# A product-key expert layer: one gather for both expert tables, and its work handled choice by choice

## The chip, the cores and the metric

The kernel runs on one core of one Trainium2 chip. The metric is the device time of one execution in microseconds, taken as a median over executions. A core has TensorE (PE: matrix multiplies, with the weight load shown apart as PEld), VectorE (DVE), ScalarE (ACT), GpSimd (POOL), SyncE (SP, which here only issues transfers), and 16 DMA engines that move data between device memory and the on-chip buffers.

## The reference, cut to what matters

Two layers of a backbone run on 128 prompt tokens and 512 latent tokens, together five blocks of 128 tokens. Each layer has a token mixer and then PEER, an expert layer with 128 x 128 = 16384 tiny experts. For every token and every one of 8 heads, two lists of 128 scores are cut to their best 16, the 256 sums of pairs are cut to the best 16, and the 16 experts so chosen give one row of `u_tab` and one of `v_tab` each:

```python
def one(xb):                                  # a block of 128 tokens
    q = (xb @ wq).reshape(PEER_BLOCK, PEER_HEADS, 2, PEER_HALF)
    s = jnp.einsum('thpd,hpnd->thpn', q, keys).astype(jnp.float32)
    s_top, i_top = lax.top_k(s, PEER_TOPK)    # PEER_TOPK = 16
    cand = s_top[:, :, 0, :, None] + s_top[:, :, 1, None, :]
    cand_idx = i_top[:, :, 0, :, None] * PEER_N_KEYS + i_top[:, :, 1, None, :]
    best, pos = lax.top_k(cand.reshape(...), PEER_TOPK)
    idx = jnp.take_along_axis(cand_idx.reshape(...), pos, axis=-1)
    g = jax.nn.softmax(best, axis=-1)
    ue = jnp.take(u_tab, idx, axis=0)         # rows of 1024 float32 = 4 KB
    ve = jnp.take(v_tab, idx, axis=0)
    act = jax.nn.gelu(jnp.einsum('td,thkd->thk', xb, ue), approximate=False)
    return jnp.einsum('thk,thkd->td', (g * act), ve)
```

Five blocks, 8 heads, 16 choices and 2 layers make 1280 choices of 128 rows each in either table.

## The kernel before, in words

The function `experts` is one stage, run once a layer. Its work is cut into 40 units, unit n being one head and one block of tokens (`where(n)`: n // 5 and n % 5). Tokens lie across the 128 partitions. A unit has 16 choices s. There are five roles, one an engine:

- PE computes queries (`ask`, one job for two blocks), scores of the two lists (`score`, three units ahead, `LEAD = 3`) and the weighted sums. `sums(n, s)` multiplies a 128 x 128 diagonal matrix, whose diagonal holds the weight of choice s for each token, with the 128 gathered v rows, and accumulates in one of two PSUM tiles `ps_y`.
- DVE picks the 16 experts of a unit in `choose(n)` (some 22 instructions, many of which wait for the one before through the semaphore `dve_steps`), takes the dot product of the gathered u row with the token's own row (line 1834), forms the weights (lines 1838, 1840) and adds the finished `ps_y` to `y_tok` (`gather_sum`, line 1742).
- ACT takes the softmax exponentials (line 1924), the gelu of a unit's 16 dot products in one instruction (line 1928), copies the next unit's token rows to PSUM (line 1899), and builds the diagonals, one a choice (line 1935).
- POOL issues the gathers, one indirect DMA of 128 rows of 4 KB at a time (line 1637). It does nothing else until the tail of the stage.
- SP issues the plain transfers: the query weights of the next head, and at the end of the stage the loads that the next stage starts with.

The order within a unit is written out by hand. DVE does the 16 dot products of unit n, waits for gelu, forms the 16 weights, runs the whole of `choose(n + 2)`, and then `gather_sum(n - 1)`; then come the dot products of unit n + 1. Only when the weights of the unit are there does ACT start on its diagonals, and PE on its sums. So the v rows of a unit are wanted one unit later than its u rows, and POOL issues them so: two gathers of u rows of unit n, two of v rows of unit n - 1, in turn. The u rows have eight slots of 4 KB a partition in two buffers named `ring`, the v rows eight in two buffers named `early`. POOL waits for `u_used` (a dot product is done) before it issues into a u slot, and for `v_used` (a sum is done) before a v slot. POOL handles its instructions strictly in order, so a wait for a slot of one kind also holds back the gathers of the other.

In the last two units DVE also works on the end of the layer between dot products (`behind_dot`: residual, layer norm). After the last unit follow the rest of that, and in the first layer the modulation of the new rows and their transposes on PE (`new_turn`) for the next stage.

## Time and profile before

| what | value |
|---|---|
| median of 3 executions | 6708.51 us (6702.12 to 6709.55) |
| span of the profiled execution | 7135.4 us |
| instructions in it | 94928 |
| mean granted clock of TensorE in it, as a share of full speed | 0.931 |
| gathered by POOL's queue | 1342.34 MB in the two expert stages |

The page gives no other time for the profiled execution than its span, so everything outside the first and last instruction is not seen. The profiled execution is 427 us longer than the median of the unprofiled ones. In the forty slices of the page (178 us each) the two expert stages are the slices 10 to 20 and 29 to 40, where GB/s is near 355; the token mixers lie before each. A line number such as L1637 is a line of the kernel. "Idle before" in brackets names what ended the wait by the semaphore events.

### The profile page before, as it was taken

Reading aid. Unit: us, or ns where it says so; the run is one execution under the profiler, and the core shown is the slowest. Engines: PE = TensorE matmul, PEld = TensorE weight load, DVE = VectorE, ACT = ScalarE, POOL = GpSimd, SP = SyncE. Lnnn points to the kernel's source line nnn. Section 1 sums busy time; section 2 is a strip of 40 time slices with the busy share of each in tenths; the row PEclk is TensorE's granted clock in tenths of the full one; section 3 lists DMA queues with packets and bytes.
Section 4 is the critical chain, followed back from the end, with each engine's and each line's share of the span. In section 5 each row is a group of like instructions: output and inputs, shape, how many; then the busy total and the mean of one; then the engine's idle time right before and its main releaser. Section 6 shows DMA issues by size and latency. Waiting matters only on the chain. (4 is left out here: it accounts for less than half of the span.)

```text
span 7135.4 us, 94928 instructions
## 1 busy us (share of the span) xinstructions
PE 5756.5 (81%) x36912; PEld 4065.6 (57%) x36912; DVE 4044.6 (57%) x8218; ACT 1880.9 (26%) x3574; POOL 2797.2 (39%) x2909
## 2 busy tenths in 40 slices
PE   7889999795777777777788899997867777777776
PEld 7779999593333333333387799986833333333332
DVE  3654334557665666566636634346576566656666
ACT  1662112412222122212226621124121222122211
POOL 0330000014666666666613300000166666666665
PEclk8999999997998999999999999999988999999999
DMA  4002121327999999999921012222389999999998
GB/s 173 17 33 84 72 75 69 144 99 287 355 354 352 361 351 358 357 357 364 387 85 39 23 72 83 75 81 90 107 329 351 357 357 357 347 355 355 353 372 318
DMA packets 425299, 1632.88 MB, mean 229 GB/s; under 512 B 47648, under 2 KB 69600, under 8 KB 412260
## 3 DMA queue, kind: packets, MB, share of 16 engines
q0 software_dynamic: 368640, 1342.34, 49.4%
q1 hardware_dynamic: 56214, 284.46, 10.9%
q8 instruction: 297, 4.87, 0.3%
q14 instruction: 148, 1.21, 0.1%
HBM read 1611.68 MB, written 17.56 MB: 228 GB/s over the span
## 5 line engine op out<-in xcount | busy, mean ns | idle before, releaser
L1984 PE MATMUL ex_ps_y<-early,peer_small 128*128 128x512 f32 x5120 | 2534.4, 643 | 887.5 <-DMA early<-in_peer_v,ex_index 626.0
L1984 PEld LDWEIGHTS ex_ps_y<-early,peer_small 128*128 128x128 f32 x5120 | 993.4, 204 | 2348.5 <-issue 1416.5
L1834 DVE CUSTOM_DVE_ANT_0 ring<-ring,ex_ps_h 128x1024 f32<-128x1024 f32 x1280 | 1510.6, 1219 | 696.3 <-DMA ring<-in_peer_u,ex_index 545.1
L1637 POOL DMA_INDIRECT early<-in_peer_v,ex_index x1280 | 1234.7, 965 | 792.8 <-issue 355.8
L1637 POOL DMA_INDIRECT ring<-in_peer_u,ex_index x1280 | 1219.8, 953 | 706.5 <-issue 369.8
L1935 ACT ACTIVATE peer_small<-ident,ex_w 128x128 f32<-128x128 f32 x1280 | 441.2, 392 | 1477.2 <-PE ex_ps_y L1984 707.7
L1117 POOL TENSOR_SCALAR ring<-ring 128x2048 f32<-128x2048 f32 x2 | 10.8, 5387 | 1623.7 <-DMA ring<-mod_rows 1623.7
L258 PE MATMUL conv_ps<-h_high,conv_wh 128*128 128x320 f32 x1024 | 317.1, 310 | 9.3 <-DVE conv_wl L156 9.3
L258 PE MATMUL conv_ps<-h_low,conv_wh 128*128 128x320 f32 x1024 | 316.6, 309 | 0.0
L258 PE MATMUL conv_ps<-h_high,conv_wl 128*128 128x320 f32 x1024 | 316.5, 309 | 0.0
L1928 ACT ACTIVATE ex_act<-ex_dot 128x16 f32<-128x16 f32 x80 | 17.2, 216 | 1116.0 <-issue 944.7
L1965 PE MATMUL ex_ps_q<-h_high,ex_wh 128*128 128x256 f32 (+1 forms) x768 | 255.4, 333 | 57.7 <-DVE h_low L156 29.4
L258 PE MATMUL rf_ps<-rf_wh,h_high 128*128 128x256 f32 x960 | 268.2, 279 | 14.0 <-DVE rf_wl L156 14.0
L258 PE MATMUL rf_ps<-rf_wl,h_high 128*128 128x256 f32 x960 | 267.7, 279 | 0.0
L258 PE MATMUL rf_ps<-rf_wh,h_low 128*128 128x256 f32 x960 | 267.6, 279 | 0.0
L1965 PE MATMUL ex_ps_q<-h_low,ex_wh 128*128 128x256 f32 (+1 forms) x768 | 238.5, 311 | 26.5 <-issue 26.2
L1965 PE MATMUL ex_ps_q<-h_high,ex_wl 128*128 128x256 f32 (+1 forms) x768 | 239.7, 312 | 24.4 <-issue 24.1
L1038 POOL TENSOR_TENSOR room<-room,rec_bounds 128x256 f32<-128x256 f32 x80 | 64.7, 809 | 437.6 <-ACT room L1032 437.3
L1965 PEld LDWEIGHTS ex_ps_q<-h_high,ex_wh 128*128 128x128 f32 x768 | 171.0, 223 | 68.5 <-issue 37.9
L156 DVE TENSOR_TENSOR rf_wl<-ring,rf_wh 128x2048 fp32r<-128x2048 f32 (+1 forms) x36 | 74.7, 2085 | 238.5 <-ACT rf_wh L285 238.5
L156 DVE TENSOR_TENSOR conv_wl<-ring,conv_wh 128x2048 fp32r<-128x2048 f32 (+1 forms) x42 | 91.7, 2188 | 203.1 <-ACT conv_wh L285 203.1
L258 PEld LDWEIGHTS conv_ps<-h_high,conv_wh 128*128 128x128 f32 x1024 | 193.5, 189 | 9.8 <-DVE conv_wl L156 9.8
(335 smaller groups left out, 12091.3 us busy)
## 6 DMA issues: line engine op xcount, KB each, us to landing
ring<-in_w_in SPq DMA_DIRECT2D x54, 2048.0 KB, 7.8
ring<-in_mod_w SPq DMA_DIRECT2D x22, 2048.0 KB, 7.6
ring<-in_w_branch SPq DMA_DIRECT2D x12, 2048.0 KB, 7.8
ring<-in_peer_u,ex_index POOLq DMA_INDIRECT x1280
early<-in_peer_v,ex_index POOLq DMA_INDIRECT x1280
room<-in_peer_wq SPq DMA_DIRECT2D x14, 1024.0 KB
ring<-in_w_out SPq DMA_DIRECT2D x4, 2048.0 KB, 8.3
room<-mod_rows SPq DMA_DIRECT2D x12, 512.0 KB, 7.9
```

The source lines that it names most:

```text
L156: return nc.vector.tensor_tensor(low, full, high.bitcast(F32), ALU.subtract)
L258: last = nc.tensor.matmul(ps[:, at:at + cols], lhs, rhs, start=k == 0 and n == 0, stop=k == KT - 1 and n == 2)
L1038: step(nc.gpsimd.tensor_tensor(kk[:, m, at], kk[:, m, at], lb[:, 1, at], ALU.mult))
L1117: step(P_.tensor_scalar(vec[:, :, 1, :], vec[:, :, 1, :], 1.0, None, ALU.add))
L1637: nc.gpsimd.indirect_dma_start(rows[slot], None, table, bass.IndirectOffsetOnAxis(ap=index[n % 4][:, s:s + 1], axis=0)).then_inc(arrived[s ...
L1834: V.tensor_tensor_reduce(out=row, in0=row, in1=ps_h[:], scale=1.0, scalar=0.0, op0=ALU.mult, op1=ALU.add, accum_out=dot[n % 2][:, s:s + 1] ...
L1928: act.activation(act_v[n % 2][:], dot[n % 2][:], ACT.Gelu).then_inc(gelu_done, 1)
L1935: act.activation(diag[s % DIAGS], ident[:], ACT.Copy, scale=wgt[n % 2][:, s:s + 1]).then_inc(diag_ready, 1)
L1965: last = nc.tensor.matmul(ps_q[:, a, 0:width], w[h % 2][:, k, w_cols], h_split[x][:, k, toks], start=k == 0 and m == 0, stop=k == KT - 1 a ...
L1984: last = nc.tensor.matmul(ps_y[n % 2][:, c:c + 512], diag[s % DIAGS], v_row[s % V_SLOTS][:, c:c + 512], start=s == 0, stop=s == TOPK - 1)
```

## The change

The two tables are joined on the host into one, `peer_uv`, whose row holds the u row and then the v row of an expert: 8 KB. A choice takes one gather instead of two. The sixteen slots of 4 KB become eight of 8 KB in the same four half buffers; a slot is taken from the issue of its gather until its sum is done on PE, so POOL waits for `v_used` alone. `choose` is cut into 16 parts, and part s of `choose(n + 2)` stands behind the dot product s of unit n (parts 0 and 1 both behind the second). The softmax is divided by its sum ahead of time (`soften` on ACT, `shares` on DVE). Gelu, weight and diagonal are made choice by choice on ACT: three instructions for each dot product, each waiting for the one before. PE's query job is cut in two, its scores come one choice later, and the v sums of a unit run right behind the dot products of the same unit rather than one unit later. At the end of the stage the loads for the next one and the transposes move behind the last sums.

```diff
-        U_SLOTS = V_SLOTS = DIAGS = 8
-        u_row, v_row = ([room[:].rearrange("p k n -> p (k n)")[:, s * D:(s + 1) * D] for room in rooms for s in range(4)] for rooms in (ring, early))
+        SLOTS = DIAGS = 8
+        pair_row = [room[:].rearrange("p k n -> p (k n)")[:, s * 2 * D:(s + 1) * 2 * D] for room in (*ring, *early) for s in range(2)]
+        u_row, v_row = ([row[:, side * D:(side + 1) * D] for row in pair_row] for side in range(2))
...
-                def gather(rows, arrived, table, n, s):
-                    slot = s % len(rows)
-                    nc.gpsimd.indirect_dma_start(rows[slot], None, table, bass.IndirectOffsetOnAxis(
-                        ap=index[n % 4][:, s:s + 1], axis=0)).then_inc(arrived[slot], 16)
-
-                for n in range(units + 1):
-                    if n < units:
-                        pool.wait_ge(routed, n + 1)
-                    for s in range(0, TOPK, 2):
-                        if n < units:
-                            if TOPK * n + s >= U_SLOTS:
-                                pool.wait_ge(u_used, TOPK * n + s + 2 - U_SLOTS)
-                            pool.sem_inc(going, 1)
-                            for j in (s, s + 1):
-                                gather(u_row, u_in, T["peer_u"], n, j)
-                        if n:
-                            if TOPK * (n - 1) + s >= V_SLOTS:
-                                pool.wait_ge(v_used, TOPK * (n - 1) + s + 2 - V_SLOTS)
-                            pool.sem_inc(going, 1)
-                            for j in (s, s + 1):
-                                gather(v_row, v_in, T["peer_v"], n - 1, j)
+                for n in range(units):
+                    pool.wait_ge(routed, n + 1)
+                    for s in range(TOPK):
+                        if TOPK * n + s >= SLOTS:
+                            pool.wait_ge(v_used, TOPK * n + s + 1 - SLOTS)
+                        pool.sem_inc(going, 1)
+                        nc.gpsimd.indirect_dma_start(pair_row[s % SLOTS], None, T["peer_uv"], bass.IndirectOffsetOnAxis(
+                            ap=index[n % 4][:, s:s + 1], axis=0)).then_inc(uv_in[s % SLOTS], 16)
...
+                def choose(n, part):
+
+                    def chosen(step, ins):
+                        ins.then_inc(dve_steps, 1)
+                        assert step <= CHOICE_STEPS
+
+                    def behind(step):
+                        dve.wait_ge(dve_steps, n * CHOICE_STEPS + step)
+
+                    full = [P, 2, TOPK, TOPK]
+                    lo = 0 if part < 4 else 8
+                    if part == 0:
+                        dve.wait_ge(scored, n + 1)
+                        V.tensor_copy(lists[:], ps_s[:, 0:2 * P].rearrange("p (a n) -> p a n", a=2)).then_inc(listed, 1)
+                    if part == 1:
+                        dve.wait_ge(listed, n + 1)
+                    if part == 3:
+                        behind(2)
+                    if part in (1, 3):
+                        dve.sem_inc(picking, 1)
+                        lo = 0 if part == 1 else 8
...
+                    if part == 15:
+                        behind(14)
+                        chosen(15, V.scalar_tensor_tensor(num[:, 0], num[:, 0], float(P), num[:, 1], ALU.mult, ALU.add))
+                        behind(15)
+                        V.tensor_scalar(index[n % 4][:], num[:, 0], base[:, bass.ds(l, 1)], None, ALU.add).then_inc(routed, 1)
+
+                def shares(n):
+                    dve.wait_ge(soft_done, n + 1)
+                    if n >= 2:
+                        dve.wait_ge(weighed, TOPK * (n - 1))
+                    V.reciprocal(total[n % 2][:], total[n % 2][:]).then_inc(recip_done, 1)
+                    dve.wait_ge(recip_done, n + 1)
+                    V.tensor_scalar(share[n % 2][:], soft[n % 2][:], total[n % 2][:], None, ALU.mult).then_inc(share_ready, 1)
...
-                        row = u_row[s % U_SLOTS]
-                        dve.wait_ge(u_in[s % U_SLOTS], (l * units + n) * 32 + 16 * (s // U_SLOTS + 1))
+                        row = u_row[s % SLOTS]
+                        dve.wait_ge(uv_in[s % SLOTS], (l * units + n) * 32 + 16 * (s // SLOTS + 1))
                         V.tensor_tensor_reduce(out=row, in0=row, in1=ps_h[:], scale=1.0, scalar=0.0, op0=ALU.mult,
-                                               op1=ALU.add, accum_out=dot[n % 2][:, s:s + 1]).then_inc(u_used, 1)
+                                               op1=ALU.add, accum_out=dot[n % 2][:, s:s + 1]).then_inc(dotted, 1)
+                        if n == 0 and s == 1:
+                            head_low_of(4)
+                            shares(0)
+                        if n + 2 < units:
+                            if s == 1:
+                                choose(n + 2, 0)
+                            if s:
+                                choose(n + 2, s)
+                        if s == 7 and n + 1 < units:
+                            shares(n + 1)
+                        if n == 0 and s == 9:
+                            low(1)
+                        if s == 11 and b == NB - 1 and h + 2 < PH:
+                            low(h + 2)
                         behind_dot(n, s)
...
-                    dve.wait_ge(gelu_done, n + 1)
-                    V.reciprocal(total[n % 2][:], total[n % 2][:]).then_inc(recip_done, 1)
-                    dve.wait_ge(recip_done, n + 1)
-                    V.scalar_tensor_tensor(wgt[n % 2][:], act_v[n % 2][:], total[n % 2][:], soft[n % 2][:], ALU.mult, ALU.mult).then_inc(w_ready, 1)
-                    if n == 0:
-                        head_low_of(4)
-                        low(1)
-                    if n + 2 < units:
-                        choose(n + 2)
                     if n and n < units - 1:
                         gather_sum(n - 1)
...
+                def soften(n):
+                    act.wait_ge(centred_done, n + 1)
+                    if n >= 2:
+                        act.wait_ge(share_ready, n - 1)
+                    act.activation(soft[n % 2][:], centred[n % 4][:], ACT.Exp, accum_out=total[n % 2][:]).then_inc(soft_done, 1)
...
+                soften(0)
                 for n in range(units):
                     h, b = where(n)
-                    act.wait_ge(routed, n + 1)
-                    act.activation(soft[n % 2][:], centred[n % 4][:], ACT.Exp, accum_out=total[n % 2][:])
-                    if n == units - 1:
-                        roots(3, 0, 3)
-                    act.wait_ge(u_used, TOPK * (n + 1))
-                    act.activation(act_v[n % 2][:], dot[n % 2][:], ACT.Gelu).then_inc(gelu_done, 1)
                     if n + 1 < units:
-                        rows_of(n + 1)
-                    act.wait_ge(w_ready, n + 1)
+                        soften(n + 1)
                     for s in range(TOPK):
-                        if TOPK * n + s >= DIAGS:
-                            act.wait_ge(v_used, TOPK * n + s + 1 - DIAGS)
-                        act.activation(diag[s % DIAGS], ident[:], ACT.Copy, scale=wgt[n % 2][:, s:s + 1]).then_inc(diag_ready, 1)
-                        if s == TOPK // 2 - 2:
-                            if n and n + LEAD < units and where(n + LEAD)[1] % 2 == 0:
-                                turn(n + LEAD)
-                        if s == TOPK // 2:
-                            if b == 2 and h + 2 < PH:
-                                high(h + 2)
+                        r, at = TOPK * n + s, slice(s, s + 1)
+                        act.wait_ge(dotted, r + 1)
+                        if s == TOPK - 1 and n + 1 < units:
+                            rows_of(n + 1)
+                        act.activation(act_v[n % 2][:, at], dot[n % 2][:, at], ACT.Gelu).then_inc(gelu_done, 1)
+                        if s == 0:
+                            act.wait_ge(share_ready, n + 1)
+                        act.wait_ge(gelu_done, r + 1)
+                        act.activation(wgt[n % 2][:, at], act_v[n % 2][:, at], ACT.Copy, scale=share[n % 2][:, at]).then_inc(weighed, 1)
+                        act.wait_ge(weighed, r + 1)
+                        if r >= DIAGS:
+                            act.wait_ge(v_used, r + 1 - DIAGS)
+                        act.activation(diag[s % DIAGS], ident[:], ACT.Copy, scale=wgt[n % 2][:, at]).then_inc(diag_ready, 1)
+                        if s == 9 and n and n + LEAD < units and where(n + LEAD)[1] % 2 == 0:
+                            turn(n + LEAD)
+                        if s == 10 and b == 2 and h + 2 < PH:
+                            high(h + 2)
+                        if s == 12 and n == units - 1:
+                            roots(4, 0, 4)
...
-                    pe.wait_ge(v_in[s % V_SLOTS], (l * units + n) * 32 + 16 * (s // V_SLOTS + 1))
+                    pe.wait_ge(uv_in[s % SLOTS], (l * units + n) * 32 + 16 * (s // SLOTS + 1))
                     pe.wait_ge(diag_ready, TOPK * n + s + 1)
                     for c in (0, 512):
-                        last = nc.tensor.matmul(ps_y[n % 2][:, c:c + 512], diag[s % DIAGS], v_row[s % V_SLOTS][:, c:c + 512], start=s == 0, stop=s == TOPK - 1)
+                        last = nc.tensor.matmul(ps_y[n % 2][:, c:c + 512], diag[s % DIAGS], v_row[s % SLOTS][:, c:c + 512], start=s == 0, stop=s == TOPK - 1)
...
-                        if s == 2 and n and n + LEAD < units and where(n + LEAD)[1] % 2 == 0:
-                            ask(n + LEAD)
-                        if s == TOPK - 4 and n + LEAD < units:
+                        if s in (2, 5) and n and n + LEAD < units and where(n + LEAD)[1] % 2 == 0:
+                            ask(n + LEAD, (0,) if s == 2 else (1,))
+                        if s == TOPK - 3 and n + LEAD < units:
                             score(n + LEAD)
                         sums(n, s)
-                        if goes_on and n == units - 1 and s in (8, 11):
-                            new_turn((s - 8) // 3)
-                for b in range(2, NB) if goes_on else ():
+                for b in range(NB) if goes_on else ():
...
-        "peer_u": a["peer_u"].reshape(DEPTH * EXPERTS, D), "peer_v": a["peer_v"].reshape(DEPTH * EXPERTS, D),
+        "peer_uv": np.concatenate([a["peer_u"], a["peer_v"]], axis=-1).reshape(DEPTH * EXPERTS, 2 * D),```

The order of the instructions on POOL, in the middle of the first expert stage. Before (`ring` holds u rows, `early` v rows, `ex_index` the row numbers of a unit):

```order
L1637 DMA ring_6<-in_peer_u,ex_index_396 128x1024 x2
L1637 DMA early_387<-in_peer_v,ex_index_395 128x1024 x2
L1637 DMA ring_6<-in_peer_u,ex_index_396 128x1024 x2
L1637 DMA early_387<-in_peer_v,ex_index_395 128x1024 x2
L1637 DMA ring_7<-in_peer_u,ex_index_396 128x1024 x2
```

And in the changed kernel:

```order
L1643 DMA ring_6<-in_peer_uv,ex_index_388 128x2048 x2
L1643 DMA ring_7<-in_peer_uv,ex_index_388 128x2048 x2
L1643 DMA early_379<-in_peer_uv,ex_index_388 128x2048 x2
L1643 DMA early_380<-in_peer_uv,ex_index_388 128x2048 x2
L1643 DMA ring_6<-in_peer_uv,ex_index_388 128x2048 x2
```

Two kinds of gathers of two neighbouring units became one kind of one unit, half as many and twice as wide.

On DVE, at the end of a unit before: the last dot products (L1834, two rows each), the weights, and the start of the whole choice:

```order
L1834 ISA ring_7,ex_dot_403<-ring_7,ex_ps_h 128x1024
L1834 ISA ex_dot_403 128x1
L1838 RECIPROCAL ex_total_409<-ex_total_409 128x1
L1840 SCALAR_TENSOR_TENSOR ex_w_411<-ex_act_405,ex_total_409,ex_soft_407 128x16
L1674 COPY peer_small<-ex_ps_s 128x256
L1679 MAX ex_top<-peer_small 128x8 x2
L1683 MAX_INDEX ex_topi<-ex_top,peer_small 128x8
L1685 MATCH_REPLACE peer_small<-ex_top,peer_small 128x128
L1683 MAX_INDEX ex_topi<-ex_top,peer_small 128x8
L1685 MATCH_REPLACE peer_small<-ex_top,peer_small 128x128
```

And in the changed kernel around the seam of two units, where L1876 is the dot product and L1776 the finished sum of a unit:

```order
L1735 TENSOR_REDUCE ex_num<-peer_small 128x32
L1876 ISA early_380,ex_dot_395<-early_380,ex_ps_h 128x1024
L1876 ISA ex_dot_395 128x1
L1738 SCALAR_TENSOR_TENSOR ex_num<-ex_num 128x16
L1740 TENSOR_SCALAR ex_index_389<-ex_num,ex_base 128x16
L1776 COPY main<-ex_ps_y_417 128x1024
L1876 ISA ring_6,ex_dot_394<-ring_6,ex_ps_h 128x1024
L1876 ISA ex_dot_394 128x1
L1876 ISA ring_6,ex_dot_394<-ring_6,ex_ps_h 128x1024
L1876 ISA ex_dot_394 128x1
L1672 COPY peer_small<-ex_ps_s 128x256
```

The block of the choice between two units is gone; between two dot products stand at most four instructions of it.

On ACT, across a unit's end before (L1928 gelu, L1899 the token rows, L1935 the diagonals):

```order
L1935 ACTIVATE peer_small<-ident,ex_w_410 128x128 x7
L1924 ACT_TABLE_LOAD
L1924 ACTIVATE ex_soft_407,ex_total_409<-ex_centred_401 128x16
L1928 ACT_TABLE_LOAD
L1928 ACTIVATE ex_act_405<-ex_dot_403 128x16
L1899 ACTIVATE ex_ps_h<-room_2 128x1024
```

And in the changed kernel (L1979 gelu, L1983 weight, L1987 diagonal of one choice, L1947 the exponentials):

```order
L1941 ACTIVATE ex_ps_h<-room_2 128x1024
L1979 ACTIVATE ex_act_397<-ex_dot_395 128x1
L1983 ACTIVATE ex_w_405<-ex_act_397,ex_share_403 128x1
L1987 ACTIVATE peer_small<-ident,ex_w_405 128x128
L1947 ACT_TABLE_LOAD
L1947 ACTIVATE ex_soft_399,ex_total_401<-ex_centred_393 128x16
L1979 ACT_TABLE_LOAD
```

One gelu of 16 values became 16 of one value, with a weight instruction behind each; the two table loads of a unit are still two.

## Rows read from the trace of the kernel before

**Rows 1.** The page: busy time by engine.

```profile
PE 5756.5 (81%) x36912; PEld 4065.6 (57%) x36912; DVE 4044.6 (57%) x8218; ACT 1880.9 (26%) x3574; POOL 2797.2 (39%) x2909
```

**Rows 2.** Windows (start:end, length, busy by engine, clock, DMA share, GB/s): both gather stretches.

```profile
1648.00:3572.00 1924.00, 1439.30 (x3820) 676.79 (x3821) 1226.69 (x2855) 403.25 (x913) 1235.16 (x1282) 0.92 0.95 359
5188.00:7106.00 1918.00, 1428.47 (x3793) 670.22 (x3793) 1217.27 (x2837) 402.75 (x914) 1220.60 (x1276) 0.92 0.94 357
```

**Rows 3.** DMA queues in 1648:3572: packets, MB, share.

```profile
q0 software_dynamic: 184293, 671.09, 91.8%
q1 hardware_dynamic: 8976, 17.83, 2.6%
```

**Rows 4.** Windows inside one unit, 2309 to 2353.

```profile
2309.00:2315.00 6.00, 4.60 (x11) 1.82 (x10) 1.82 (x7) 0.62 (x2) 1.88 (x2) 1.00 1.02 408
2315.00:2318.00 3.00, 2.01 (x5) 0.57 (x3) 2.58 (x9) 2.04 (x7) 1.88 (x2) 1.00 0.58 176
2318.00:2324.00 6.00, 3.97 (x8) 1.35 (x8) 5.90 (x12) 0.49 (x2) 4.18 (x5) 1.00 0.87 308
2331.00:2353.00 22.00, 16.81 (x40) 6.90 (x40) 9.00 (x16) 5.31 (x10) 15.06 (x16) 0.99 1.02 408
```

**Rows 5.** Timeline of POOL: start, length, line, [idle before <-releaser].

```profile
2310.31 0.94 POOL L1637 DMA_INDIRECT ring<-in_peer_u,ex_index  x1 [0.30 <-issue]
2315.55 0.94 POOL L1637 DMA_INDIRECT early<-in_peer_v,ex_index  x1 [4.31 <-PE ex_ps_y L1984]
```

**Rows 6.** Timeline of DVE in the same unit: last dot, weights, choice, sum, first dot.

```profile
2301.78 1.22 DVE L1834 CUSTOM_DVE_ANT_0 ring<-ring,ex_ps_h 128x1024 f32<-128x1024 f32 x1
...
2303.64 0.42 DVE L1674 COPY peer_small<-ex_ps_s 128x256 f32<-128x256 f32 x1
...
2311.90 0.18 DVE L1687 CAST ex_topf<-ex_topi 128x32 f32<-128x32 uint32 x1 [4.52 <-remote]
...
2319.41 1.21 DVE L1742 TENSOR_TENSOR main<-main,ex_ps_y 128x1024 f32<-128x1024 f32 x1
2320.54 1.22 DVE L1834 CUSTOM_DVE_ANT_0 ring<-ring,ex_ps_h 128x1024 f32<-128x1024 f32 x1
```

**Rows 7.** Timeline of ACT in the next unit.

```profile
2334.70 1.28 ACT L1928 ACT_TABLE_LOAD   x1
2347.59 0.21 ACT L1928 ACTIVATE ex_act<-ex_dot 128x16 f32<-128x16 f32 x1 [11.61 <-issue]
2347.72 1.01 ACT L1899 ACTIVATE ex_ps_h<-room 128x1024 f32<-128x1024 f32 x1
```

**Rows 8.** Timelines: DVE, one hop from ACT; ACT, a diagonal.

```profile
7082.28 0.16 DVE L1838 RECIPROCAL ex_total<-ex_total 128x1 f32<-128x1 f32 x1 [0.28 <-ACT ex_act L1928]
...
2330.10 0.40 ACT L1935 ACTIVATE peer_small<-ident,ex_w 128x128 f32<-128x128 f32 x1 [5.79 <-issue]
```

**Rows 9.** Timeline of PE: the last sums of the program, back to back.

```profile
7089.64 22.91 PE L1984 MATMUL ex_ps_y<-early,peer_small 128*128 128x512 f32 x53
```

**Rows 10.** Windows: plain loads of 16 KB a partition, at the program's start.

```profile
5.00:20.00 15.00, 7.55 (x140) 6.45 (x144) 8.95 (x4) 2.12 (x2) 0.00 (x0) 1.00 1.01 429
```

**Rows 11.** Windows where TensorE had idled.

```profile
2375.00:2378.00 3.00, 0.00 (x0) 0.00 (x0) 3.00 (x6) 0.00 (x0) 2.31 (x3) 1.00 1.06 410
2378.00:2381.00 3.00, 2.67 (x4) 0.68 (x4) 1.09 (x3) 0.00 (x0) 2.17 (x3) 0.74 1.04 422
2381.00:2384.00 3.00, 1.21 (x3) 0.66 (x3) 1.42 (x4) 2.89 (x5) 2.39 (x3) 0.50 1.03 420
```

**Rows 12.** DVE and POOL at the ends of the stages.

```profile
3594.99 1.22 DVE L1781 TENSOR_TENSOR main<-main,ring 128x1024 f32<-128x1024 f32 x1
3599.34 1.22 DVE L156 TENSOR_TENSOR h_low<-ex_ps_h,h_high 128x1024 fp32r<-128x1024 f32 x1 [3.12 <-ACT h_high L1947]
...
7120.01 1.28 DVE L1775 SCALAR_TENSOR_TENSOR room<-room,ex_root,room 128x1024 f32<-128x1024 f32 x1
...
L1664 POOL TENSOR_TENSOR main<-main,ring x2: 3200/3212/3224, 3568.7 to 3582.4; 128x1024 f32<-128x1024 f32 x2
```

154 lines of the change are left out of this document (85 added, 69 removed).

## The prediction

> **What bounds the kernel now.** I read the page's busy shares first: PE 81%, DVE 57%, POOL 39% [rows 1]. No engine is full over the span, so the answer must come from a stage. The stages that the change touches are the two gather stretches. In windows over them, the DMA engines are busy 95% and 94% of 1924 and 1918 us, at 359 and 357 GB/s, while PE has 1439 us of work (36.0 us for each of 40 units), DVE 1227 (30.7) and ACT 403 (10.1) [rows 2]. 671.09 MB of the 688.9 MB moved there are gathered rows [rows 3]. That looks like a transfer limit, but the average hides two levels. Inside one unit the engines hold 408 GB/s for 22 us at a stretch, and then comes a hole: 176 GB/s for 3 us, 308 for the next 6 [rows 4]. So the transfers are the bound only in the good part of a unit, and something makes the holes.
>
> The hole has a cause in the order. POOL waited 4.31 us for a sum on PE before it could issue into a v slot, and every u gather behind it stood too [rows 5]. PE had no diagonals, since ACT's gelu waits for all 16 dot products of the unit. And DVE, after its last dot product at 2301.78, is away with weights, choice and sum until 2320.54, of which 4.52 us are a wait in the middle of the choice [rows 6]: 17.6 us without a dot product, in which eight u slots of 0.52 MB fill in 10 us and then stand full. The bound is a transfer rate of 408 GB/s with a hole of each unit in it: 16.78 MB at 408 take 41.1 us, and a stretch of 1924 us for 40 units is 48.1.
>
> **The change part by part.**
>
> Bytes stay the same: 1280 gathers of 1 MB for 2560 of half that. At the rate of the good part, 688.9 MB / 408 GB/s = 1688 us a stage. Nothing in the trace shows a gather of 8 KB rows. Plain loads of 16 KB a partition ran at 429 GB/s over 15 us [rows 10]. At that rate the stage would take 1606 us. I take 408, the row for the same queue and kind, and keep 429 as the far end; on the bad side a gather of 8 KB rows could be no faster per instruction than two of 4 KB, which is 408 again.
>
> POOL: 0.94 us a gather and 0.30 between two [rows 5], so 32 x 1.24 = 39.7 us a unit before and 19.8 now. If a row of 8 KB counts as two rows, the instruction is 1.88 us and the unit 34.9, still below 41. This is a gain in room, not in time.
>
> Dot products and choice: the instructions are the same, 30.7 us of DVE a unit. A part of the choice is at most four short instructions; the biggest pieces are some 1.3 us, and with a dot product of 1.22 [rows 6] that is 2.5 us, against 1688 / 640 = 2.64 us a choice. Waits of a part for the part before it fall behind a dot product, and so cost nothing. What is queued behind a waiting part is the next dot product, and behind that ACT, PE and the slot. I price that by the 8 slots below.
>
> ACT: 16 gelu instructions instead of one and 16 weight instructions are new. From 0.21 us for a gelu, the same for a weight, 0.40 for a diagonal and 0.28 for a hop of a semaphore [rows 7, 8], a choice takes 0.21 + 0.28 + 0.21 + 0.28 + 0.40 + 0.28 = 1.7 us, below 2.64. A copy begins right behind a gelu with no table load between [rows 7], so alternating gelu and copy brings none. Two table loads of 1.28 us a unit stay, and now stand in front of the first choice of a unit: some 3 us, once a unit.
>
> PE: a sum is four passes, 22.91 / 53 = 0.43 us each, 1.73 us [rows 9]. All its work is 36.0 us a unit, below 42, and its half jobs of queries now delay one sum by 3 us rather than by 6.
>
> Slots: a row of 8 KB is held after landing for dot product 1.22, hop 0.28, ACT 1.7 and sum 1.73, about 5 us. Eight slots go round in 8 x 2.64 = 21 us, which leaves 16 us for the transfer, so six gathers stay in flight. A stall of DVE, ACT or PE of 5 to 8 us is covered; one of 11 us would leave a hole, and a few may. That replaces what went: I see nothing late next but the transfer itself.
>
> Start of a stage: DVE does head work and all of `choose(1)` before its first dot product, while the eight slots take 20 us to fill. I add 7 us. So 1695 us a stage against 1924, a gain of 229, or 458 for both.
>
> End of a stage: before, DVE and POOL did most of the tail beside v gathers and sums of the last unit. Now the last dot product follows the last landing, and then come two normal rows, two modulations, the sum, residual 4 and the low parts, some 34 us of DVE, where it was 28 after 3572 (to 3599.34) [rows 12]; POOL's four operations of 3.2 us each and the two transposes that wait for them follow the modulations. I add 12 us in the first layer. The second layer had a drain of PE alone (22.91 us [rows 9]) and its end hangs on the same seven operations of DVE up to 7120.01 [rows 12]: plus 4. The loads for the next stage are issued some 15 us before the last sum instead of some 45, and need 10, so they are covered; if not, they cost 5.
>
> Sum: 7135.4 - 458 + 16 = about 6693 us for a profiled execution, 442 less. The median of the runs shown is 427 us less than that span, and the trace doesn't say where. If the whole execution shrinks alike, the gain is 442 x 0.94 = 415 and the time 6293. If the waits shrink and the byte-bound time can't, a stretch of before is 1924 x 0.94 = 1809, the new one 1695, and the gain 2 x 114 - 16 = 212: 6497. I take the middle, 6400.
>
> The Trainium skill speaks against all this. Its page "DMA: Bandwidth & Descriptors", section "Bandwidth", puts the limit for transfers from device memory at about 358 GB/s a core, and says that for these "the HBM side (~358) binds". The averages of 359 and 357 GB/s would be just that limit, and the change would gain nothing. But 408 GB/s over 22 us and 429 over 15 us stand in this trace [rows 4, 10], so by the rows the limit is higher for this core alone.
>
> **The rivals.**
>
> No change. The average rate is a ceiling over long stretches, and the 408 GB/s are bursts that the holes pay for. For it: both stretches agree within 0.6% [rows 2]. Against: each hole has an engine in it that waits for a slot [rows 5], which a ceiling wouldn't need. By the rule of the page this is what would come. The time would be 6708.5 + 16, or, with ends hidden, 6700.
>
> Half the gain. Some holes come back. The 4.52 us wait in the choice has no cause in the order [rows 6]; if such a stall strikes DVE, ACT and PE in turn, each a few times in two units, the eight slots run empty now and then, since every choice now goes through all three in series. The gain halves: 106 to 208, 6500 to 6600.
>
> More than forecast. Wider rows run at 429 GB/s: 82 us a stage more, 164 both, so 6240 from the middle.
>
> Slower: TensorE's clock. Where PE had idled, the granted clock fell from 1.00 to 0.50 [rows 11], the level of 1.2 GHz. Now sums come singly, 1.73 us of work and 0.9 us of pause, for 40 units. At 1.2 GHz all the time PE would need 72 us a unit against 48.1 now: 80 x 24 = 1900 us more. It decides from about a third of the time at the low level: 36 + 12 = 48. Against it: in the 22 us of 408 GB/s PE also works in pieces (16.81 of 22 us) and the clock is 0.99 [rows 4]; and a late PE has more work waiting, which fills its pauses. A small share of it would give 6750 to 6900.
>
> That the change doesn't do what it says is excluded by the order of instructions, which shows the halved gathers and the parts between dot products.
>
> **How the numbers follow.** Forecast (the holes close, rate near 408) 0.72, with its own range 6290 to 6500. More than forecast 0.10. Half the gain 0.10. No change 0.03. Slower 0.05. A difference under 0.2% (13 us) can't be told from none. Faster is 0.72 + 0.10 + 0.10 and a little of the rest, 0.92; same 0.02; slower 0.06. The range goes down half way to 6115, which is the fully scaled gain together with 429 GB/s, and up to the edge of the half gain: 6200 to 6600.
>
> **What would show it.** Right: in the gather stretches DMA share 1.0 and 400 GB/s or more in nearly every slice; stretches near 1700 us; DVE's main wait is for the landing of a row, at each choice; POOL waits mostly for sums on PE, with 640 gathers a stage of about 0.94 us. Wrong: slices near 358 GB/s with POOL never waiting would mean the ceiling; a mean clock well under 0.9 in the stretch with PE full would mean the slow rival; POOL waiting for PE while DMA share is below 0.95 would mean that eight slots are too few.

## The result

The changed kernel takes 6634.47 us (6628.62 to 6640.34, median of 4 runs), the kernel before beside it 6705.32 (6697.67 to 6709.55): ratio 0.9894, 95% interval 0.988 to 0.9908. It is faster by 71 us, 1.1%, where about 308 were forecast, and the time lies outside the range given. The profiled execution of the changed kernel has a span of 6626.6 us and a time of 6628.62: here profile and timing agree, as they did not for the kernel before, whose profiled execution was 427 us longer than the median. That gap is what the study is about. **On some occasions every execution of the kernel before takes 7103 to 7175 us (medians 7122 to 7158), on others 6697 to 6714 (medians 6702 to 6705), and by its span of 7135.4 us the profile shown ahead of the prediction belongs to the first sort.** An occasion is a set of runs of several kernels made one after another on one chip; the two sorts are called the slow and the fast level below. No profile of the kernel before was kept from the other.

The page of the changed kernel, busy time by engine and then the gather queue of the whole program (packets, MB, share of 16 engines):

```profile
PE 5624.5 (85%) x36912; PEld 3969.9 (60%) x36912; DVE 3985.8 (60%) x8216; ACT 2568.0 (39%) x6050; POOL 1574.6 (24%) x1629
...
q0 software_dynamic: 184320, 1342.26, 49.1%
```

Against [rows 1] POOL has fallen from 2797 to 1575 us (1280 instructions fewer), ACT has gained 687 us for 2476 instructions more, PE and DVE are nearly as they were.

Windows of the changed kernel over the first gather stretch (columns as in [rows 2]):

```profile
1653.00:1700.00 47.00, 35.87 (x118) 20.58 (x119) 37.93 (x106) 18.86 (x51) 20.87 (x21) 0.86 0.89 355
1700.00:3320.00 1620.00, 1332.63 (x3706) 602.70 (x3705) 1150.90 (x2747) 726.56 (x2100) 591.90 (x620) 0.97 1.01 415
3320.00:3340.00 20.00, 5.10 (x19) 3.32 (x17) 19.76 (x13) 3.33 (x3) 10.48 (x4) 0.64 0.20 80
```

The stretch is 1667 us long, not 1924 [rows 2], and 1620 us of it run at 415 GB/s with the DMA engines full. The 408 GB/s of [rows 4] were no burst. The Trainium skill's page "DMA: Bandwidth & Descriptors", section "Bandwidth", has about 358 GB/s for each of two cores that stream from the same memory domain, and a measured 425 GB/s for a 16 MB transfer on one core with its neighbour idle. This kernel runs on one core, and its trace is near the second figure, with 415 GB/s over 1620 us. The prediction took the 358 without that condition.

What DVE and POOL waited for between 2000 and 3000 us (engine, tile and line, releaser: us in total, times, longest):

```profile
DVE early L1876 <- DMA early<-in_peer_uv,ex_index: 162.7, 187, 2.1
DVE ring L1876 <- DMA ring<-in_peer_uv,ex_index: 120.4, 152, 2.1
POOL early L1643 <- PE ex_ps_y L2035: 299.5, 183, 3.7
POOL ring L1643 <- PE ex_ps_y L2035: 281.4, 159, 4.7
```

DVE waits for landings, choice by choice and never over 2.1 us; the 17.5 us without a dot product [rows 6] are gone. The same view of the kernel before:

```profile
DVE ring L1834 <- DMA ring<-in_peer_u,ex_index: 150.7, 58, 10.2
DVE peer_small L1674 <- remote: 89.9, 16, 10.6
DVE ring L1834 <- issue: 43.6, 21, 4.1
DVE ex_topf L1687 <- remote: 24.4, 7, 4.9
```

Here is the sign that the prediction had in one row only, the 4.52 us at line 1687 [rows 6]: waits whose releaser is "remote" (a signal came, but no instruction ended just before it) or "issue" (nothing that the profile shows was waited for). DVE has 182 us of them in 1000, the longest of 10.6 us. In the changed kernel it has none. That they are not waits of the order can be read at the longest. The copy at line 1674 waits for PE's scores alone (the semaphore `scored`), and PE had ended them 17 us before (timelines, windows 2004 to 2006 and 2020 to 2024):

```profile
2004.95 0.61 PE L1977 MATMUL ex_ps_s<-room 128*128 128x128 f32 x4
2022.92 0.42 DVE L1674 COPY peer_small<-ex_ps_s 128x256 f32<-128x256 f32 x1 [10.61 <-remote]
```

At each of the 16 copies with such a wait the scores had been done for 7.8 us or more. These waits are called stalls below: an engine starts late although what it waits for is done.

A choice on ACT at the end of the stage (timeline: start, length, line, [idle before <-releaser]), and POOL at its start, with the hole that eight full slots make before the first sum:

```profile
3309.33 0.20 ACT L1979 ACTIVATE ex_act<-ex_dot 128x1 f32<-128x1 f32 x1 [1.20 <-DVE ex_dot L1876]
3309.56 0.29 ACT L1983 ACTIVATE ex_w<-ex_act,ex_share 128x1 f32<-128x1 f32 x1
3309.89 0.40 ACT L1987 ACTIVATE peer_small<-ident,ex_w 128x128 f32<-128x128 f32 x1
```

```profile
1662.74 0.94 POOL L1643 DMA_INDIRECT early<-in_peer_uv,ex_index  x1 [0.30 <-issue]
1676.94 0.94 POOL L1643 DMA_INDIRECT ring<-in_peer_uv,ex_index  x1 [13.26 <-PE ex_ps_y L2035]
```

A choice costs ACT 0.96 us from gelu to the end of the diagonal. The gather instruction takes 0.94 us as before [rows 5], for a row of 8 KB as for one of 4 KB.

### The profile page after: what moved, and what is told of

Its sections match the earlier page's. It is cut to its first block and busy times, and to the rows that moved or that the text cites. A ratio compares the mean times of both kernels' runs of the same rounds, so it can differ in the third digit from the quotient of the medians.

```text
span 6626.6 us, 97627 instructions
## 1 busy us (share of the span) xinstructions
PE 5624.5 (85%) x36912; PEld 3969.9 (60%) x36912; DVE 3985.8 (60%) x8216; ACT 2568.0 (39%) x6050; POOL 1574.6 (24%) x1629
## 3 DMA queue, kind: packets, MB, share of 16 engines
q0 software_dynamic: 184320, 1342.26, 49.1%
## 5 line engine op out<-in xcount | busy, mean ns | idle before, releaser
L2035 PE MATMUL ex_ps_y<-ring,peer_small 128*128 128x512 f32 x2560 | 1261.5, 636 | 290.9 <-ACT peer_small L1987 290.7
L2035 PE MATMUL ex_ps_y<-early,peer_small 128*128 128x512 f32 x2560 | 1222.7, 608 | 292.4 <-ACT peer_small L1987 287.6
L2035 PEld LDWEIGHTS ex_ps_y<-ring,peer_small 128*128 128x128 f32 x2560 | 488.6, 201 | 1021.7 <-issue 1020.3
L1876 DVE CUSTOM_DVE_ANT_0 early<-early,ex_ps_h 128x1024 f32<-128x1024 f32 x640 | 780.5, 1221 | 516.9 <-DMA early<-in_peer_uv,ex_index 516.5
L2035 PEld LDWEIGHTS ex_ps_y<-early,peer_small 128*128 128x128 f32 x2560 | 451.4, 190 | 972.7 <-issue 972.4
L1876 DVE CUSTOM_DVE_ANT_0 ring<-ring,ex_ps_h 128x1024 f32<-128x1024 f32 x640 | 780.5, 1220 | 407.5 <-DMA ring<-in_peer_uv,ex_index 400.2
L1643 POOL DMA_INDIRECT ring<-in_peer_uv,ex_index x640 | 623.8, 975 | 1151.0 <-PE ex_ps_y L2035 913.7
L1979 ACT ACTIVATE ex_act<-ex_dot 128x1 f32<-128x1 f32 x1280 | 256.9, 201 | 1595.8 <-DVE ex_dot L1876 1594.9
L1643 POOL DMA_INDIRECT early<-in_peer_uv,ex_index x640 | 606.7, 948 | 1021.5 <-PE ex_ps_y L2035 984.6
L1987 ACT ACTIVATE peer_small<-ident,ex_w 128x128 f32<-128x128 f32 x1280 | 514.0, 402 | 42.0
L1983 ACT ACTIVATE ex_w<-ex_act,ex_share 128x1 f32<-128x1 f32 x1280 | 376.8, 294 | 46.4
L156 DVE TENSOR_TENSOR rf_wl<-ring,rf_wh 128x2048 fp32r<-128x2048 f32 (+1 forms) x36 | 74.7, 2086 | 242.4 <-ACT rf_wh L285 242.4
```

What stands on the lines that cost most here:

```text
L156: return nc.vector.tensor_tensor(low, full, high.bitcast(F32), ALU.subtract)
L1643: nc.gpsimd.indirect_dma_start(pair_row[s % SLOTS], None, T["peer_uv"], bass.IndirectOffsetOnAxis(ap=index[n % 4][:, s:s + 1], axis=0)).th ...
L1876: V.tensor_tensor_reduce(out=row, in0=row, in1=ps_h[:], scale=1.0, scalar=0.0, op0=ALU.mult, op1=ALU.add, accum_out=dot[n % 2][:, s:s + 1] ...
L1979: act.activation(act_v[n % 2][:, at], dot[n % 2][:, at], ACT.Gelu).then_inc(gelu_done, 1)
L1983: act.activation(wgt[n % 2][:, at], act_v[n % 2][:, at], ACT.Copy, scale=share[n % 2][:, at]).then_inc(weighed, 1)
L1987: act.activation(diag[s % DIAGS], ident[:], ACT.Copy, scale=wgt[n % 2][:, at]).then_inc(diag_ready, 1)
```

## The experiments

Four questions, in the order in which they came up. Each kernel is compared with the kernel before on the same occasion. Edits are shortened to the lines that matter. Where dots and sums run on 64 of 1024 columns, or a choice is left out, the text of the expectation or of the edit says so.

**1. Which part of the change brings the gain?** All four on one occasion, on which the kernel before took 7157.78 us (7137.2 to 7175.48).

Two 4 KB gathers a choice, all of the new order kept:

```diff
-  indirect_dma_start(pair_row[s % SLOTS], None, T["peer_uv"], ...index[n % 4][:, s:s + 1]).then_inc(uv_in[s % SLOTS], 16)
+  for row, table in ((u_row, "peer_u"), (v_row, "peer_v")):
+      indirect_dma_start(row[s % SLOTS], None, T[table], ...index[n % 4][:, s:s + 1]).then_inc(uv_in[s % SLOTS], 16)
```

> The changed kernel with its gathers undone alone: each choice takes two gathers of 4 KB rows from the two tables into the halves of its slot; the order of all engines stays. Three theories of why 442 us were expected and 71 came. P: the profile itself slows a stream of 4 KB packets (it records each), the holes of the profiled execution of before are not there in timed runs, and the stage of before stood at a transfer limit already; then this kernel's profiled span is far above its timed runs (6850 or more against 6650 to 6700). O: the order made the difference in the profile, and a timed run of before has smaller holes for another reason; then the profiled span is within 30 us of the timed runs, and both are near 6640. R: the 71 us are the rate of 8 KB rows (415 against about 405 GB/s); then the timed runs are at 6690 to 6710, whatever the profile says.

Measured: 7116.54 us (7108.66 to 7124.15), ratio 0.9954 (0.9938 to 0.997). None of the three theories has that time. Theory P falls besides: the profiled execution took 7108.66 us, in the range of the others, and for every kernel run here it is within 21 us of the median. So profiling doesn't make the gap.

The changed kernel with dots and sums on 64 of 1024 columns (`row[:, 0:64]`, `v_row[..][:, 0:64]`), once with 8 KB gathers and once with 4 KB gathers as above:

> The changed kernel with dot products and sums over 64 of the 1024 columns only (it leaves out the rest of both), so that no engine but the DMA ones is near its limit in the stage. All theories: the transfer limit for 8 KB rows, 6570 to 6630 timed, if the changed kernel (6634) stands at it. If it is below 6500, the changed kernel is held by its engines and not by transfers.

> The same with two gathers of 4 KB rows a choice (the same columns left out). P and R: the limit for 4 KB rows is higher than for 8 KB rows, by 30 to 80 us of timed time, and before (6705) stands within 30 us above it. O: as floor8 within 10 us, so that before has 60 us and more of holes in timed runs. P besides: the profiled span is above the timed runs by 200 us or more, though nothing but transfers can bound it.

Measured: 6623.17 (6610.37 to 6632.86) with 8 KB, 7073.17 (7060.05 to 7085.98) with 4 KB; ratios 0.9259 (0.9238 to 0.9281) and 0.9893 (0.9869 to 0.9916). The first is as expected; the second is 370 us or more above what any theory had.

The kernel before with the choice left out from the third unit on, so that DVE is hardly away between two units:

```diff
+  if n >= 2:
+      V.tensor_scalar(centred[n % 4][:], best[:], best[:, 0:1], None, ALU.subtract)
+      for _ in range(CHOICE_STEPS):
+          dve.sem_inc(dve_steps, 1)
+      V.tensor_scalar(index[n % 4][:], num[:, 0], base[:, bass.ds(l, 1)], None, ALU.add).then_inc(routed, 1)
+      return
```

> The kernel before with the choice between two units left out from the third unit on (it takes the experts of unit 1 again, and computes none of the rest), so the block of 11 to 16 us on DVE between dot products shrinks to some 2 us. P: timed within 20 us of 6705, since the block is hidden there. O: 40 us or more below 6705. In the profile the holes shrink in both, or stay if they are the profile's own: below 6800 if the order makes them even there, above 7000 if it doesn't.

Measured: 7127.19 (7115.75 to 7137.79), ratio 0.996 (0.9942 to 0.9978). DVE's stalls are what they were, 182.3 us of 1000 against 182.0, and the profiled time stayed above 7000 us, which the expectation kept for holes that the order doesn't make.

Windows 2000 to 3000 us of the four: `a4k`, `floor4`, `floor8`, `b_nochoice`:

```profile
2000.00:3000.00 1000.00, 773.02 (x2070) 362.16 (x2071) 617.84 (x1517) 401.42 (x1149) 649.12 (x681) 0.92 0.96 361
```

```profile
2000.00:3000.00 1000.00, 345.76 (x1390) 299.96 (x1390) 281.37 (x1521) 391.31 (x1143) 653.38 (x688) 0.54 0.96 365
```

```profile
2000.00:3000.00 1000.00, 386.78 (x1598) 331.68 (x1598) 322.00 (x1745) 453.69 (x1314) 391.48 (x392) 0.54 1.01 418
```

```profile
2000.00:3000.00 1000.00, 756.34 (x2067) 358.74 (x2066) 463.32 (x804) 216.60 (x485) 636.01 (x674) 0.92 0.94 358
```

With less than half of the work on PE and DVE (346 and 281 us for 773 and 618) the transfer stays at 365 GB/s as long as there are two gathers a choice, and is at 418 with one, so the low average is no ceiling on the transfers either. The new order with the old gathers gains 0.5%, the old order without its block on DVE 0.4%. The changed kernel itself was not run beside these; on another slow occasion it takes 6633 (question 2). So on this level the single gather is nearly the whole gain, and the holes that the prediction laid to the order have another cause.

**2. Is it the width of the row, or the number of gathers?** One occasion, kernel before 7121.52 us (7108.74 to 7162.69). First the changed kernel itself:

> The changed kernel as it is, beside the kernel before on this chip. Theory W (the wide gather is worth some 480 us wherever gathers of 4 KB run at 360 GB/s): on a chip where the kernel before takes 7120 to 7180 us this takes 6620 to 6650, ratio 0.925 to 0.932; on a chip where the kernel before takes 6705 it takes 6634, ratio 0.989. Theory Z (the changed kernel has the same two levels as the kernel before): the ratio stays at 0.989 on every chip, so about 7080 where the kernel before takes 7158.

Measured: 6632.69 (6625.63 to 6638.29), ratio 0.931 (0.9272 to 0.9349). The changed kernel shows no second level: 6634 where the kernel before takes 6705, 6633 where that takes 7122. DVE's stalls in it on this slow occasion sum to 1.7 us of 1000.

Then, on 64 of 1024 columns, a second gather beside each 8 KB gather, of rows of 64 B from a small table, with the same indices:

```diff
   indirect_dma_start(pair_row[s % SLOTS], None, T["peer_uv"], ...)
+  indirect_dma_start(tiny[s % SLOTS][:], None, T["peer_tiny"], ...index[n % 4][:, s:s + 1]).then_inc(uv_in[s % SLOTS], 16)
```

> The kernel with dots and sums on 64 of 1024 columns and 8 KB gathers (6623 us), and beside each of its gathers a second one of rows of 64 B from a small table: as many gather instructions and descriptors as with 4 KB gathers, 0.8% more bytes. Theory I (twice the gather instructions on GpSimd leave no room to make up for a stall: 64 of 1.24 us in a unit of 41 us): 7030 to 7100 us, as with 4 KB gathers. Theory S (the size of the row decides, not the number of gathers): 6620 to 6690, the descriptors of 64 B adding at most 1% to the transfers.

(The 64 in it should read 32: a unit has 16 choices.) Measured: 7032.14 (7029.73 to 7045.14). All the bytes but 0.8% move in rows of 8 KB, and the time is near that of 4 KB gathers. The width of the row is refuted as the cause, the number of gathers stands.

Four slots in place of eight with the 4 KB gathers, so that half as many are in flight:

> The same kernel with two 4 KB gathers a choice (7073 us with eight slots, so sixteen gathers in flight) and four slots: eight gathers of 4 KB in flight, as many gathers as the changed kernel has, half its bytes. Theory C (sixteen gathers outstanding stall GpSimd's queue and with it the other engines): 6620 to 6700, the stalls gone. Theories S and I: 7060 to 7200, no better, perhaps worse because fewer bytes are in flight.

Measured: 7108.32 (7105.31 to 7126.36), against 7073 with eight slots on another occasion. Fewer in flight is no cure; theory C falls.

The changed kernel with half the bytes, one 4 KB gather a choice:

> The changed kernel with half the bytes: rows of 4 KB that hold the first 512 columns of both experts, one gather a choice; the dot and the two matmuls of a choice keep their sizes. With a transfer of 4 KB at 360 GB/s it takes 23 us of a unit, so the engines set the unit. Theory S (rows of 4 KB bring stalls of 2 to 8 us on all engines wherever they are): the stalls are seen here too, DMA below its rate in over 10% of the slices though asked for half, 5500 to 6000 us. Theory I: no such stalls, GpSimd with room, 5100 to 5500 us. Both: with the transfers out of the way the next bound of a unit is DVE, ScalarE and TensorE at some 29 to 33 us.

Measured: 5931.92 (5915.66 to 5935.37). No wait on "remote" appears on DVE or POOL between 2000 and 3000 us, so 1280 gathers of 4 KB are as quiet as 1280 of 8 KB. The time by itself lies in the range of theory S (5500 to 6000), and the 5500 us of theory I were too low by 430; it is the trace that speaks for I, without the stalls and with PE as the bound, at 946 of 1000 us busy.

```profile
2000.00:3000.00 1000.00, 946.38 (x2836) 472.76 (x2836) 883.25 (x2115) 555.08 (x1607) 469.95 (x476) 0.98 0.78 265
```

**3. The number of rows, or of instructions?** On a first occasion the kernel before took 6704.37 us, the other level, on which the question can't be put. All on 64 of 1024 columns: the second gather with 16 rows in place of 128, the second gather beside every other choice only (`if s % 2:`), and, with no second gather, two small multiplications on GpSimd behind each gather.

```diff
-  indirect_dma_start(tiny[s % SLOTS][:], None, T["peer_tiny"], ...index[n % 4][:, s:s + 1])
+  indirect_dma_start(tiny[s % SLOTS][0:16, :], None, T["peer_tiny"], ...index[n % 4][0:16, s:s + 1])
```

> As the kernel with a second gather of 64 B rows beside each 8 KB gather (7032 us; 6623 without it), but the second gather fetches 16 rows on 16 partitions instead of 128: as many gather instructions on GpSimd (32 a unit), but 9 descriptors for every 8 as without it, instead of 16. Theory I (what counts is that GpSimd issues without a pause, about 1.24 us each): about 7030, unless the smaller gather is issued much faster, then in proportion. Theory D (what counts is the number of rows, thus descriptors and packets): 6640 to 6690.

> The second gather of 128 rows of 64 B only beside every other choice: 24 gathers in a unit instead of 16 (6623 us) or 32 (7032). Theory D (each gather of 128 rows costs its descriptors, in proportion): half of the 409 us, 6810 to 6850. Theory I (GpSimd has to be without a pause; 24 x 1.24 = 29.8 us of a unit of 41): 6620 to 6680.

> No second gather; in its place two multiplications of a tile of 128 columns on GpSimd behind each gather, each waited for, by the row of 0.81 us for 256 columns some 0.4 us each with their waits 1.0 to 1.2 us: GpSimd as full as with 32 gathers a unit, with 16 gathers. Theory I (a full GpSimd, whatever it does): 6950 to 7100 us. Theory D or any theory of the gathers themselves: 6620 to 6660.

Measured: 6635.43 (6616.6 to 6644.28), 6644.24 (6632.91 to 6647.05) and 6908.75 (6907.8 to 6921.68). The last one, which neither theory has, tells nothing of the stalls: it has none on DVE, and it was not run on the slow level. It is slow for a reason of its own. Its gathers stand 2.72 us apart, 0.98 for the gather and the rest for the two multiplications and their waits, so GpSimd's own chain needs 43.5 us for the 16.78 MB of a unit, which is 386 GB/s; 383 were measured.

On a second occasion the kernel before took 7128.56 us (7103.09 to 7155.4):

> Again the second gather of 128 rows of 64 B beside each 8 KB gather (7032 us on chip 11). Where the kernel before takes 7120 to 7160: 7030 to 7050. Where it takes 6705: if the level belongs to the chip and not to the kernel, 6640 to 6700.

> Again the second gather with 16 rows (6635 us on chip 4). Where the kernel before takes 7120 to 7160: 7000 to 7050 if the number of gather instructions counts (theory I), 6640 to 6690 if the number of rows does (theory D). Where it takes 6705: 6635 again, which tells nothing new.

> Again the second gather beside every other choice (6644 us on chip 4). Where the kernel before takes 7120 to 7160: 6810 to 6850 if each gather has a price (theory D), 6640 to 6680 if GpSimd has to be without a pause (theory I). Where it takes 6705: 6644 again.

> Again the changed kernel with two 4 KB gathers a choice (7117 us on chip 13). Where the kernel before takes 7120 to 7160: 7080 to 7120. Where it takes 6705: if the order of the steps is what is left of the gain there, 6640 to 6660; if the wide row is, 6690 to 6710.

Measured: 7039.77 (7027.11 to 7046.68) with 128 rows, **7040.67 (7019.95 to 7053.75) with 16 rows**, 6672.38 (6663.62 to 6675.4) beside every other choice, and 7085.07 (7067.15 to 7094.81; ratio 0.9936, 0.9918 to 0.9955) for the changed kernel with two 4 KB gathers. Sixteen rows cost as much as 128: it is not rows, packets or bytes but gather instructions on GpSimd. Half as many extra ones cost 49 us over the 6623 without any (another occasion), not half of 417. The same kernel took 6644 on the other level, so 28 of the 49 belong to the slow one.

The same kernel, the one with 16 rows, on the two occasions: windows of the fast and of the slow one, and then the three largest of DVE's stalls in the slow one, where they sum to 286.6 us (in the fast one there are none).

```profile
2000.00:3000.00 1000.00, 383.37 (x1586) 328.17 (x1587) 322.07 (x1738) 453.28 (x1309) 709.32 (x776) 0.54 1.01 415
```

```profile
2000.00:3000.00 1000.00, 343.77 (x1372) 299.29 (x1373) 282.40 (x1540) 394.28 (x1156) 632.40 (x691) 0.53 0.94 368
```

```profile
DVE ex_topf L1701 <- remote: 57.3, 15, 6.2
DVE ex_best L1707 <- remote: 44.0, 11, 5.8
DVE ring L1879 <- issue: 28.7, 20, 2.1
```

One such moment in its slow execution, by the timelines of DVE and POOL:

```profile
2055.15 0.08 DVE L1879 DVE_READ_ACCUMULATOR2_ANT ex_dot<- 128x1 f32 x1 [0.53 <-issue]
...
2056.96 0.95 POOL L1644 DMA_INDIRECT ring<-in_peer_uv,ex_index  x1 [3.80 <-issue]
...
2058.22 0.85 POOL L1646 DMA_INDIRECT ex_tiny<-in_peer_tiny,ex_index  x1 [0.30 <-issue]
...
2060.77 0.18 DVE L1701 CAST ex_topf<-ex_topi 128x32 f32<-128x32 uint32 x1 [5.53 <-remote]
...
2060.86 0.95 POOL L1644 DMA_INDIRECT ring<-in_peer_uv,ex_index  x1 [1.79 <-remote]
```

The CAST waits only for DVE's own last index search, which ended at 2054.50, and still starts after 5.5 us of idling; POOL's next gather, late too, starts 0.09 us after it. The core as a whole doesn't stand still: POOL issued two gathers while DVE waited. With every other choice doubled, on the slow level, there are stalls of DVE too, but shorter:

```profile
DVE early L1880 <- issue: 47.0, 25, 2.9
DVE ring L1880 <- issue: 30.3, 20, 2.3
```

There GpSimd is busy 563 of 1000 us and has room to make up for them. With 32 gathers it needs 32 x 1.24 = 39.7 us of a unit of some 41, and what is lost stays lost. But room isn't all: the stalls themselves grow with the gathers. DVE's sum to 7.3 us of 1000 with 16 gathers a unit (`floor8`), to 77.3 with 24 and to 286.6 with 32, all on the slow level, and the longest are 1.9, 2.9 and 8.6 us.

**4. Are the holes that are left worth closing?** Three mends together: the query weights in runs of 8 KB, the choices of the first units dealt out between the first dot products, the modulations that GpSimd had at the end (blocks 2 and 3) on DVE.

```diff
-  return T["peer_wq"][bass.ds(l, 1), h // 2]...[:, :, (h % 2) * HALF:(h % 2 + 1) * HALF]
+  return T["peer_wq"][bass.ds(l, 1), h]...
-  for part in range(TOPK):
-      choose(1, part)
+  choose(1, 0)                          # the others: two behind each dot product of unit 0
-  POOL_BLOCKS = (2, 3)
+  POOL_BLOCKS = ()
```

> The changed kernel with three mends: the query weights laid out so that a partition's share is one run of 8 KB instead of 1 KB pieces (their load, 25.5 us to land, held the gathers at 314 to 396 GB/s for some 20 us in a stretch, seven stretches a stage); choices of units 1 and 2 dealt out between the first dot products instead of ahead of them (GpSimd waited 13.3 us at the start of a stage); the last modulation on VectorE instead of GpSimd. If transfers at 415 to 420 GB/s are the bound and these are the holes in them: 6560 to 6620 us against 6633. If the holes are hidden: 6625 to 6640.

> The changed kernel again, beside the one with the three mends. 6625 to 6640 us on any chip; ratio to the kernel before 0.989 where that takes 6705, 0.925 to 0.932 where it takes 7120 to 7160.

> The three mends (query weights in runs of 8 KB, choices of the first units between the first dot products, last modulation on VectorE) on the same chip as the changed kernel: 8 to 14 us below it if the 6623 of chip 4 holds, 0.12 to 0.21%; no difference if it was the chip.

Measured: 6623.32 (6622.8 to 6626.51) on one occasion; then side by side, with 6701.68 for the kernel before, the changed kernel 6626.34 (6620.9 to 6636.28; ratio 0.988, 0.9863 to 0.9896) and the mended one 6628.92 (6622.1 to 6631.82; 0.9885, 0.9869 to 0.9902). No difference that can be told, and no mend has brought the 6560 to 6620 us hoped for. The windows 1660 to 1700 us, the changed kernel and then the mended one, show the start fuller (391 and 406 GB/s), and the next stage starts some 4 us sooner:

```profile
1660.00:1700.00 40.00, 30.02 (x88) 14.55 (x87) 32.24 (x81) 18.86 (x51) 16.63 (x16) 0.91 0.97 391
```

```profile
1660.00:1700.00 40.00, 29.76 (x84) 14.40 (x83) 35.11 (x102) 22.10 (x56) 14.41 (x14) 0.91 0.99 406
```

Four us are 0.06% of the time. GpSimd's wait at the start of the stage, 12.56 us in the changed kernel beside it, is still 11.16: there it waits for the first sum with all eight slots taken. No version beats the changed kernel.

## Why the prediction was wrong

**The step that failed** is the one from the profiled execution to the median. The prediction had 442 us less for a profiled execution, found the median 427 us under the profile "and the trace doesn't say where", and carried 212 to 415 us of the gain over to it. But the 427 us were, nearly all, the holes that the change was to close. That is shown by the levels (the kernel before at 7122 and 6705, the changed kernel at 6633 and 6634) and by the kernel with 16-row gathers, which has stalls at 7041 us and none at 6635; of the kernel before itself there is no trace at 6705. On the occasions of 6705 us it has no room for such holes: the stretch is 35 us longer than the changed kernel's 1667 if the 71 us fall on the two alike, and 688.9 MB in 1702 us are 405 GB/s, nearly the 408 of the good part. By this estimate, what could be gained there was what lies between 405 and 415 GB/s. By the profile's own level the forecast was good: 6693 expected, and on a slow occasion the ratio is 0.931 to 7121.52 us, 489 less rather than 442. The text had both numbers and could have asked whether 427 and 442, nearly the same, were the same thing; it treated the gap as a scale instead.

**Right.** Rate: 408 was taken, 415 measured over 1620 us; over 688.9 MB that is 1660 for 1688 us, 28 us a stage better, a third of the 82 us of the rival with wider rows; whether the width of the row does it isn't shown. Stretch: 1667 for 1695. Gather instruction 0.94 us, ACT below 2.64 us a choice (0.96 us where 1.7 with hops were taken), eight slots enough: no wait of DVE over 2.1 us in 1000 us. TensorE's clock: 0.97 mean in the stretch, and with PE three fifths empty it fell to 0.54 (the windows with 64 columns above) at no cost in time, 6623 for 6633. The end of the first stage: from the last landing, near 3316, to the next stage's first matmul at 3368.26 are 52 us, where before it was 41 from the 3572 at which the stretch of [rows 2] ends to 3612.7: 11 more, 12 forecast.

Two sums are slightly off: the second stretch was 1918 us, so the profiled gain is 452 rather than 458, and the 6115 at the far end of the range doesn't follow (6293 less two times 82 is 6129). Neither changes the outcome.

**Wrong in the mechanism.** The hole was laid to DVE being away and POOL being held. Both are in the rows, but neither is what costs the time on the slow level: without the choice on DVE 0.4% came back, with the new order and the old gathers 0.5 to 0.6%. That the profiled level came out near 6693 is luck in this respect, since the change happened to halve the gather instructions too. POOL's halved work was priced as "a gain in room, not in time"; on the slow level the halved number of gather instructions is nearly the whole gain. The 4.52 us on "remote" had been read as a wait that "has no cause in the order", and was put to a rival of 0.10; it was the only row shown of what does cost the time, and the waits over 1000 us, asked for, have 25 on "remote" on DVE alone.

**Open.** What holds engines for up to 10 us on the slow occasions though their condition is met, and what makes an occasion slow: the same chip was at 7158 on one occasion and at 6702 on a later one. That the stalls come with the number of gather instructions a unit is shown by dose (16, 24 and 32: 6623, 6672, 7040 us, the first on another occasion); how, isn't. Whether another kind of work on GpSimd does it too was tried on the fast level only, so it isn't shown that gathers alone do it. And no kernel with 4 KB gathers in the new order fell on a fast occasion, so how the 71 us divide between row width and order there is argued from rates alone. The number of gathers has little part in them: on such occasions the kernels with 24 and 32 gathers a unit took 6644 and 6635 us.

## What to carry to other kernels

When a profiled execution and the median differ by several per cent, ask first whether they belong to the same level, and forecast for the level of the median. Look over a long window at waits whose releaser the profile doesn't know; an engine that waits for itself is not held by the order. Where indirect gathers are issued back to back, join tables so that one instruction fetches both rows: with half the gather instructions this kernel was at one time on every occasion, where the other lost 6 to 7% on some.

## What the runs showed of the hardware

A gather instruction of 128 rows holds GpSimd for 0.94 to 0.98 us in the mean and is followed by 0.30 us when nothing is waited for, with rows of 64 B, 4 KB and 8 KB alike; with 16 rows it takes 0.85 us. So on GpSimd the number of instructions is the price, not what they fetch. With rows of 8 KB one core moved 415 to 418 GB/s for 1000 us and more, 98% of it gathered. On the slow level a wait can end long after its condition is met: PE's scores were done 17 us before DVE's copy of them began. The kernel with 16-row gathers took 6635 and 7041 us on two occasions, while kernels with 16 gathers of 8 KB a unit, the one with added multiplications aside, took 6623 to 6634 on the five occasions on which they were run.
